# Row maxima of both heads in one VectorE operation, and both sink columns in one write, in a block of four attentions

## The chip, the cores and the metric

The kernel runs on one core of a Trainium2 chip. A core has a matrix engine (TensorE, PE in the profile; its weight loads are PEld), a vector engine (VectorE, DVE), a scalar engine (ScalarE, ACT), a general engine (GpSimd, POOL) and a queue that starts transfers (SyncE, SP). The engines run their own lists of instructions and meet through semaphores: a wait names a semaphore and a count, and other engines' instructions add to it as they end. PSUM is the memory that TensorE writes, eight banks of 512 float32 for each of 128 partitions. The metric is the device time of one execution in microseconds (us), the median of several.

## The reference

Two transformer blocks on 512 tokens of width 1024, in float32. Cut to the attentions, which are what the change touches, and to how the blocks are chained:

```python
# first block
p = jax.nn.softmax(jnp.where(causal, s, -jnp.inf), axis=-1)      # differential attention
a = p[:, :, 0] - lam * p[:, :, 1]
...
p = masked_softmax(s, m)                                          # NSA: selected blocks, window
o = gb[..., 0:1] * o_cmp + gb[..., 1:2] * o_slc + gb[..., 2:3] * o_win
...
x = x + mixed @ w_out[l]
x = x + jnp.square(jax.nn.relu(h @ w_mlp_up[l])) @ w_mlp_down[l]

# second block
logits = logits + ci[..., :, None] - c_k[..., None, :]            # forgetting attention
p = jax.nn.softmax(jnp.where(causal, logits, -jnp.inf), axis=-1)
h = h + (o * jax.nn.silu(gate)) @ w_out_a[i]
...
sink = broadcast_to(sinks, logits.shape[:-1] + (1,))              # windowed attention with sinks
probs = jax.nn.softmax(jnp.concatenate([logits, sink], axis=-1), axis=-1)[..., :-1]
```

Every softmax subtracts the maximum of its row (one query, one head) before the exponential. In the windowed attention each head has one more logit, its sink, which counts in the maximum and in the sum and is dropped then.

## The kernel before

The kernel is written by hand for each engine, with semaphores between them; the order of instructions on an engine is the order in the code. Between long stretches of weight products (line 1421, three products per tile of a high and a low part) come four attentions: DIFF (8 units), NSA (16 units: 8 pairs of heads, each for selected blocks and for the window), FOX (8 units, forgetting) and SWA (8 units, window of 128 with sinks). A unit is two heads, on 512 queries in four tiles of 128. The tiles are taken from the last (`t` = 3, `idx` = 0) to the first, since the last has the widest rows: 512, 384, 256 and 128 keys in DIFF, NSA and FOX, and 256, 256, 256 and 128 in SWA, plus one sink column.

Each engine has a function `attend(a)`, which runs `step(m, ...)` for a unit `m` through `over_units`: the first three units written out, the middle in a loop of two units a turn, and the rest written out. In one step the engines work on the scores of unit `m` and on the values of the unit before it, `b`. For one tile and both heads:

- TensorE, `scores_of`: the products of queries and keys of both heads into two banks, `PS[:, 2 * (idx % 2) + h]`; then for head 0 and for head 1 the mask product (line 1659), with the decay (line 1655) in FOX and the band (1658) in SWA ahead of it. Each head's last product adds one to `s`. Before a tile it waits for the exponentials of the tile that had the same banks.
- VectorE, `maxima`: for head 0, then for head 1, a wait for `s`, in SWA a write of the head's sink into the column behind the scores (line 975) and a wait for that, and the negated row maximum into `NM` (line 978), which adds one to `mx`.
- ScalarE, `exps` (lines 611 to 616): for each head a wait for `mx` and the exponential into `PB` with the row sum into `LS`; the second one adds one to `e`.
- VectorE, `norms` (line 983): the reciprocals of both heads' sums. GpSimd scales the probabilities with them (line 1369).
- TensorE, `turn_p` (line 1678), a unit later: the scaled probabilities transposed into banks 4 and 5. ScalarE (line 625) and, outside DIFF, VectorE (line 1003) copy them to `PT`, and `values_of` (line 1693 in DIFF, 1698 in the others) multiplies them with the values into bank 6.
- For the next unit, `turn` (line 1712) transposes queries and keys into bank 7, ScalarE rounds them (line 633), VectorE takes the rest (line 1008). In FOX and SWA VectorE gates a finished output (line 1026), ScalarE rounds it (line 638), and VectorE takes the rest (line 1032).

The order in a step, which decides who waits for whom: TensorE has scores 3, values 0 of the unit before `b`, transposes 3 of `b`, scores 2, values 3, transposes 2, scores 1, queries of the next unit, values 2, transposes 1, keys of the next unit, scores 0, values 1, transposes 0. ScalarE has exponentials 3, in FOX and SWA the rounding of an output, copies 3 and 2 of `b`, exponentials 2, rounding of queries, exponentials 1, copy 1, rounding of keys, exponentials 0, copy 0. VectorE has maxima 3, the finished output, reciprocals 0 and copy 3 of `b`, maxima 2, reciprocals 3, copy 2, the rest of an output, maxima 1, reciprocals 2, rest of queries, copy 1, maxima 0, rest of keys, reciprocals 1, copy 0.

## Time and profile before

| | us |
|---|---|
| three runs | 1947.2, 1955.84, 1944.85 |
| their median | 1947.2 |
| the profiled execution's own time | 1947.98 |
| its span, from the first to the last instruction | 1946.2 |
| busy in the span: PE / DVE / ACT / POOL | 1759.8 / 892.9 / 705.7 / 366.0 |
| mean granted clock of TensorE | 0.94 |
| DIFF (from 222 to 317 us) | 95 |
| NSA's attention in units (from 595 to 777 us) | 182 |
| FOX (from 1487 to 1609 us) | 122 |
| SWA (from 1790 to 1890 us) | 100 |

The last four rows are stretches of the profiled execution's span that I cut at the first and last score product of each attention. "Busy" is time in which an engine works on an instruction; a row's idle time is what the engine stood before its instructions, with the engine and line whose end released it. A granted clock of 1.00 is TensorE's level of 2.4 GHz, 0.50 that of 1.2 GHz.

### The profile page before, as it was taken

Reading aid. Unit: us, or ns where it says so; the run is one execution under the profiler, and the core shown is the slowest. Engines: PE = TensorE matmul, PEld = TensorE weight load, DVE = VectorE, ACT = ScalarE, POOL = GpSimd, SP = SyncE. Lnnn points to the kernel's source line nnn. Section 1 sums busy time; section 2 is a strip of 40 time slices with the busy share of each in tenths; the row PEclk is TensorE's granted clock in tenths of the full one; section 3 lists DMA queues with packets and bytes.
Section 4 is the critical chain, followed back from the end, with each engine's and each line's share of the span. In section 5 each row is a group of like instructions: output and inputs, shape, how many; then the busy total and the mean of one; then the engine's idle time right before and its main releaser. Section 6 shows DMA issues by size and latency. Waiting matters only on the chain.

```text
span 1946.2 us, 24116 instructions
## 1 busy us (share of the span) xinstructions
PE 1759.8 (90%) x8846; PEld 1348.3 (69%) x8846; DVE 892.9 (46%) x1569; ACT 705.7 (36%) x1525; POOL 366.0 (19%) x490
## 2 busy tenths in 40 slices
PE   2999888999978998997999999989998998798878
PEld 2888656887664554886888888868775546686547
DVE  2485274224544665344342234231662653353661
ACT  3322365122135666323341233132323552433550
POOL 4251042102213655010000000000111440020320
PEclk9999797999987999999999999989998998898899
DMA  5223222323102221432223232322222112132211
GB/s 128 85 87 122 73 76 65 108 87 108 44 12 52 58 67 30 153 108 87 66 89 105 88 107 87 108 65 86 87 82 71 55 34 88 64 108 68 63 41 68
DMA packets 148049, 154.85 MB, mean 80 GB/s; under 512 B 48972, under 2 KB 90172, under 8 KB 147960
## 3 DMA queue, kind: packets, MB, share of 16 engines
q1 hardware_dynamic: 141768, 152.74, 24.8%
q0 software_dynamic: 992, 0.86, 0.3%
q10 hardware_dynamic: 5200, 0.02, 0.3%
q8 instruction: 61, 1.00, 0.2%
q14 instruction: 28, 0.23, 0.0%
HBM read 123.15 MB, written 2.15 MB: 64 GB/s over the span
## 4 chain that ended last, share of the span: by engine, by line
PE 83%; DVE 7%; ACT 6%; issue 3%; ACTq 1%; POOL 0%; DVEq 0%; POOLq 0%
PE ps L1421 61%; PE ps L1649 4%; PE ps L1678 3%; PE ps L1698 3%; PE ps L1712 2%; ACT pb L614 2%; PE ps L1659 2%; DVE qkt L1008 1%; ACTq L476 1%; DVE nm L978 1%; ACT qkt L633 1%; PE ps L1655 1%; PE ps L1549 1%; PE ps L1519 1%; PE ps L1620 1%
## 5 line engine op out<-in xcount | busy, mean ns | idle before, releaser
L1421 PE MATMUL ps<-spl,ht 128*128 128x512 f32 x2496 | 583.0, 396 | 31.5 <-DVE spl L787 16.3
L1421 PEld LDWEIGHTS ps<-spl,ht 128*128 128x128 f32 x2496 | 477.8, 192 | 135.0 <-issue 13.6
L787 DVE TENSOR_TENSOR spl<-raw,spl 128x1024 fp32r<-128x1024 f32 x196 | 253.5, 1336 | 568.5 <-ACT spl L494 568.5
L494 ACT ACTIVATE spl<-raw 128x1024 fp32r<-128x1024 f32 x196 | 196.3, 1052 | 640.0 <-PE ps L1421 639.1
L1421 PE MATMUL ps<-ht,spl 128*128 128x512 f32 x1536 | 351.8, 391 | 2.0 <-DVE spl L787 2.0
L1421 PEld LDWEIGHTS ps<-ht,spl 128*128 128x128 f32 x1536 | 289.9, 189 | 63.2 <-issue 2.9
L614 ACT ACTIVATE pb<-ps,nm 128x512 f32<-128x512 f32 (+5 forms) x320 | 161.4, 513 | 85.9 <-DVE nm L978 85.9
L978 DVE TENSOR_REDUCE nm<-ps 128x1 f32<-128x512 f32 (+5 forms) x320 | 140.0, 467 | 81.9 <-PE ps L1659 78.7
L1421 PE MATMUL ps<-spl,uu 128*128 128x512 f32 x768 | 174.4, 389 | 0.0
L1421 PEld LDWEIGHTS ps<-spl,uu 128*128 128x128 f32 x768 | 144.1, 188 | 29.9
L1649 PE MATMUL ps<-qkt 64*128 64x256 f32 (+2 forms) x960 | 126.4, 372 | 15.8 <-issue 7.0
L1331 POOL TENSOR_TENSOR sq<-qkv 128x2048 f32<-128x2048 f32 (+1 forms) x15 | 51.5, 3435 | 451.2 <-ACT qkv L528 436.6
L1678 PEld LDWEIGHTS ps<-idf,pb 128*128 128x128 f32 x672 | 74.9, 144 | 62.4 <-issue 51.2
L1369 POOL TENSOR_TENSOR pb<-pb,rr 128x256 f32<-128x256 f32 (+3 forms) x128 | 81.5, 660 | 191.3 <-DVE rr L983 191.2
L1649 PEld LDWEIGHTS ps<-qkt 64*128 64x128 f32 x960 | 80.0, 208 | 49.5 <-issue 40.8
L1369 POOL TENSOR_TENSOR pb<-pb,rg 128x512 f32<-128x512 f32 (+3 forms) x160 | 112.8, 721 | 7.5
L1698 PE MATMUL ps<-pt,stv 128*64 128x256 f32 (+3 forms) x512 | 94.1, 446 | 20.3 <-ACT pt L625 11.0
L1678 PE MATMUL ps<-idf,pb 128*128 128x128 f32 x672 | 109.9, 289 | 0.0
L625 ACT ACTIVATE pt<-ps 128x256 f32<-128x256 f32 (+3 forms) x160 | 67.8, 424 | 86.5 <-PE ps L1678 86.1
L1008 DVE TENSOR_TENSOR qkt<-ps,qkt 128x512 fp32r<-128x512 f32 x80 | 54.9, 686 | 94.6 <-ACT qkt L633 94.6
L1421 PE MATMUL ps<-ys,spl 128*128 128x512 f32 x384 | 88.9, 394 | 0.0
L1379 POOL MEMSET nws<- 128x2048 f32 x2 | 3.6, 1807 | 440.0 <-PE ps L1421 440.0
(244 smaller groups left out, 1562.8 us busy)
## 6 DMA issues: line engine op xcount, KB each, us to landing
raw<-w_in SPq DMA_DIRECT2D x30, 1024.0 KB, 5.2
raw<-w_mlp_up SPq DMA_DIRECT2D x16, 1024.0 KB, 5.2
raw<-w_mlp_down SPq DMA_DIRECT2D x16, 1024.0 KB, 5.1
raw<-w_in_a SPq DMA_DIRECT2D x16, 1024.0 KB, 5.3
stq<-qkv SPq DMA_DIRECT2D x56, 256.0 KB, 2.7
raw<-w_in_b SPq DMA_DIRECT2D x8, 1024.0 KB, 5.1
stq<-qkv SPq DMA_DIRECT2D x48, 128.0 KB, 2.5
raw<-w_proj_diff SPq DMA_DIRECT2D x4, 1024.0 KB, 5.1
```

Of the source, the lines that this page charges most:

```text
L494: act.activation(SPL[:, n % 2, HI, 2 * k:2 * k + 2], RAW[:, n % 2, 2 * k:2 * k + 2], ACT.Copy).then_inc(hi_done, 1)
L614: last = act.activation(p, PS[:, 2 * (idx % 2) + h, 0:w], ACT.Exp, bias=NM[:, m.slot, h, t:t + 1], accum_out=LS[:, m.slot, h, t:t + 1])
L625: act.activation(PT[odd][:, 0 if a.is_diff else idx % 2, 0:w], PS[:, 4 + odd, 0:w], ACT.Copy)\
L787: dve.tensor_tensor(SPL[:, n % 2, LO, 2 * k:2 * k + 2], RAW[:, n % 2, 2 * k:2 * k + 2], SPL[:, n % 2, HI, 2 * k:2 * k + 2].bitcast(F32), A ...
L978: dve.tensor_reduce(top, bank[:, 0:w + a.sink], AX.X, ALU.max, negate=True).then_inc(s["mx"], 1)
L1008: dve.tensor_tensor(QKT[:, m.slot, i, LO], PS[:, 7], QKT[:, m.slot, i, HI].bitcast(F32), ALU.subtract)\
L1331: pool.tensor_tensor(SQ[:, :, 0:w], QKV[:, :, col:col + w], QKV[:, :, col:col + w], ALU.mult)\
L1369: last = pool.tensor_tensor(p, p, by[:, m.slot, h, t:t + 1].to_broadcast([P, w]), ALU.mult)
L1421: last = pe.matmul(PS[:, b0 + b], left[:, x], right[:, y], start=(kt == 0 and i == 0), stop=(kt == UK * g["units"] - 1 and i == 2))
L1649: pe.matmul(PS[:, 2 * (idx % 2) + h, 0:w], QKT[r, m.slot, 0, x, P * t:P * t + P], QKT[r, m.slot, 1, y, P * a.first_key(t):P * t + P], star ...
L1678: last = pe.transpose(bank[:, P * i:P * i + P], PB[:, m.slot, h, o:o + P], IDF[:])
L1698: last = pe.matmul(PS[HD * h:HD * h + HD, 6, cols], STV[:, m.slot, j, v], PT[h][:, idx % 2, 0:w], start=(idx == 0 and not (a.is_nsa and m. ...
```

## The change

`maxima` waits once, for the scores of both heads, writes both sinks with one operation (two columns in two banks), and takes both maxima with one reduction over a 128 x 2 x w view of the two banks, into two places of `NM`. `mx` counts one for each step instead of two. `exps` waits once, ahead of both exponentials. TensorE's wait for the last maxima of an attention counts accordingly.

```diff
@@ ScalarE, exps
                     w = a.width(t) + a.sink
+                    act.wait_ge(s["mx"], 4 * m.n + idx + 1)
                     for h in range(2):
-                        act.wait_ge(s["mx"], 8 * m.n + 2 * idx + h + 1)
                         p = PB[:, m.slot, h, a.offset(t):a.offset(t) + w]
@@ VectorE, maxima
                     w = a.width(t)
-                    for h in range(2):
-                        n = 8 * m.n + 2 * idx + h + 1
-                        bank, top = PS[:, 2 * (idx % 2) + h], NM[:, m.slot, h, t:t + 1]
-                        dve.wait_ge(s["s"], n)
-                        if a.is_swa:
-                            dve.tensor_scalar(bank[:, w:w + 1], SINK[:, bass.ds(2 * m.n + h, 1)], 1.0, None, ALU.mult)\
-                               .then_inc(sink_in, 1)
-                            dve.wait_ge(sink_in, n)
-                        dve.tensor_reduce(top, bank[:, 0:w + a.sink], AX.X, ALU.max, negate=True).then_inc(s["mx"], 1)
+                    n = 4 * m.n + idx + 1
+                    banks = PS[:, 2 * (idx % 2):2 * (idx % 2) + 2]
+                    dve.wait_ge(s["s"], 8 * m.n + 2 * idx + 2)
+                    if a.is_swa:
+                        dve.tensor_scalar(banks[:, :, w], SINK[:, bass.ds(2 * m.n, 2)], 1.0, None, ALU.mult)\
+                           .then_inc(sink_in, 1)
+                        dve.wait_ge(sink_in, n)
+                    dve.tensor_reduce(NM[:, m.slot, :, t], banks[:, :, 0:w + a.sink], AX.X, ALU.max, negate=True)\
+                       .then_inc(s["mx"], 1)
@@ TensorE, banks_left
-                pe.wait_ge(s["mx"], 8 * a.units)
+                pe.wait_ge(s["mx"], 4 * a.units)
```

The lists of TensorE, GpSimd and SyncE are the same in both kernels. Each row below is one instruction; REGISTER_ALU and ISA rows are the sequencer's own work for counts and addresses in a loop.

ScalarE at the start of a turn of NSA's loop, from the exponentials of tile 3 (128x512) over the copies of the unit before (L625) to the exponentials of tile 2:

```order
-L612 ISA
-L614 ACTIVATE pb,ls<-ps,nm 128x512
-L612 REGISTER_ALU
-L614 ACTIVATE pb,ls<-ps,nm 128x512
-L622 REGISTER_ALU
-L625 ACTIVATE pt_66<-ps 128x128
...
+L611 ISA
+L614 ACTIVATE pb,ls<-ps,nm 128x512 x2
+L622 REGISTER_ALU
+L625 ACTIVATE pt_66<-ps 128x128
```

The wait between the two exponentials is gone, and the one ahead of the first is for both heads; the copy still follows behind both.

VectorE at the same place, from the maxima of tile 3 to the finished output (L1018):

```order
 L332 UNCONDITIONAL_BRANCH
 L332 ISA
-L978 TENSOR_REDUCE nm<-ps 128x1
-L973 REGISTER_ALU
-L978 TENSOR_REDUCE nm<-ps 128x1
+L977 TENSOR_REDUCE nm<-ps 128x2
 L1015 ISA
 L1018 ISA
```

Two reductions of one row each have become one of two rows.

VectorE in SWA's loop, from the rest of an output (L1032) over the maxima of tile 1 to the reciprocals (L983) and the rest of the queries (L1007, L1008):

```order
 L1032 TENSOR_TENSOR ht<-yt,ht 128x512
-L973 REGISTER_ALU
-L975 TENSOR_SCALAR ps<-sink 128x1
-L978 TENSOR_REDUCE nm<-ps 128x1
-L973 REGISTER_ALU
-L975 TENSOR_SCALAR ps<-sink 128x1
-L978 TENSOR_REDUCE nm<-ps 128x1
-L982 REGISTER_ALU
+L972 REGISTER_ALU
+L974 TENSOR_SCALAR ps<-sink 128x2
+L976 REGISTER_ALU
+L977 TENSOR_REDUCE nm<-ps 128x2
```

Four instructions of VectorE have become two.

## Rows read from the trace of the kernel before

**Rows 1.** The page's costliest groups: busy us, mean ns | idle before, releaser

```profile
L978 DVE TENSOR_REDUCE nm<-ps 128x1 f32<-128x512 f32 (+5 forms) x320 | 140.0, 467 | 81.9 <-PE ps L1659 78.7
```

**Rows 2.** Stretches: PE, PEld, DVE, ACT, POOL busy; clock; DMA; GB/s

```profile
249.84:298.96 49.12, 41.66 (x290) 26.80 (x291) 37.95 (x96) 34.55 (x110) 20.56 (x40) 1.00 0.26 78
660.63:734.71 74.08, 71.62 (x533) 41.66 (x534) 51.24 (x130) 48.40 (x155) 44.33 (x84) 1.00 0.25 62
1531.55:1581.69 50.14, 50.03 (x338) 27.79 (x338) 34.36 (x81) 30.60 (x93) 23.99 (x32) 1.00 0.21 61
1821.82:1875.50 53.68, 43.89 (x379) 27.44 (x380) 39.29 (x141) 33.26 (x115) 21.51 (x40) 1.00 0.21 52
```

**Rows 3.** VectorE's reductions by shape: busy us, mean ns of one

```profile
L978 DVE TENSOR_REDUCE nm<-ps 128x1 f32<-128x512 f32 x64 | 41.4, 687 | 26.4 <-PE ps L1659 26.3
L828 DVE TENSOR_REDUCE ss<-sq 128x16 f32<-128x1024 f32 x3 | 3.6, 1212 | 1.8 <-POOL sq L1331 1.8
L1214 DVE TENSOR_REDUCE lc<-ps 128x16 f32<-128x512 f32 x4 | 2.8, 692 | 8.5 <-PE ps L1589 8.4
```

**Rows 4.** Timeline of one NSA unit: start, us, engine, line [idle before, releaser]

```profile
662.74 1.29 DVE L978 TENSOR_REDUCE nm<-ps 128x1 f32<-128x512 f32 x2 [0.36 <-PE ps L1659]
663.46 0.69 ACT L614 ACTIVATE pb<-ps,nm 128x512 f32<-128x512 f32 x1 [1.18 <-DVE nm L978]
...
664.81 0.27 ACT L625 ACTIVATE pt<-ps 128x128 f32<-128x128 f32 x1
...
665.05 1.02 DVE L978 TENSOR_REDUCE nm<-ps 128x1 f32<-128x384 f32 x2 [0.59 <-PE ps L1659]
665.13 0.20 PEld L1698 LDWEIGHTS ps<-pt,stv 128*64 128x64 f32 x4 [0.24 <-ACT pt L625]
...
666.48 0.58 ACT L614 ACTIVATE pb<-ps,nm 128x384 f32<-128x384 f32 x1
```

**Rows 5.** Timeline of one DIFF unit, the same place

```profile
290.53 1.29 DVE L978 TENSOR_REDUCE nm<-ps 128x1 f32<-128x512 f32 x2 [0.82 <-PE ps L1659]
...
292.92 0.49 PE L1693 MATMUL ps<-pt,stv 128*128 128x128 f32 x2 [0.41 <-ACT pt L625]
```

**Rows 6.** Timeline of one FOX unit, the same place

```profile
1558.79 0.23 PE L1659 MATMUL ps<-causal,idb 128*128 128x128 bf16 x1
...
1559.06 1.29 DVE L978 TENSOR_REDUCE nm<-ps 128x1 f32<-128x512 f32 x2 [0.68 <-PE ps L1659]
...
1559.27 0.23 PE L1659 MATMUL ps<-causal,idb 128*128 128x128 bf16 x1
...
1561.58 0.63 ACT L638 ACTIVATE ht<-yt 128x512 f32 x1 [0.35 <-DVE yt L1026]
...
1562.43 0.20 PEld L1698 LDWEIGHTS ps<-pt,stv 128*64 128x64 f32 x4
```

**Rows 7.** Timeline of one SWA unit, from its third step to the next one's first

```profile
1843.51 0.15 DVE L975 TENSOR_SCALAR ps<-sink 128x1 f32 x1
...
1843.70 0.43 DVE L978 TENSOR_REDUCE nm<-ps 128x1 f32<-128x257 f32 x1
...
1844.57 0.16 DVE L983 RECIPROCAL rr<-ls 128x2 f32<-128x2 f32 x1
...
1846.71 0.16 DVE L975 TENSOR_SCALAR ps<-sink 128x1 f32 x1 [1.06 <-PE ps L1659]
...
1847.51 0.68 DVE L1008 TENSOR_TENSOR qkt<-ps,qkt 128x512 fp32r<-128x512 f32 x1
...
1849.48 0.16 DVE L975 TENSOR_SCALAR ps<-sink 128x1 f32 x1 [0.90 <-PE ps L1659]
...
1850.54 0.68 DVE L1026 TENSOR_TENSOR yt<-ps,mx 128x512 f32<-128x512 f32 x1
...
1850.66 0.48 ACT L614 ACTIVATE pb<-ps,nm 128x257 f32<-128x257 f32 x1
...
1851.37 0.63 ACT L638 ACTIVATE ht<-yt 128x512 f32 x1
```

## The prediction

> **What bounds the kernel now.** I read the page first, then the table of stretches, then the timeline inside each of the four attentions. On the page the reader is to see that the 320 row maxima take 140 us of VectorE and that VectorE sat idle 81.9 us before them, nearly all of it for TensorE's scores [rows 1]: they are taken as soon as their input is there, so what they wait for and who waits for them decides, not their sum. The edit touches only the four attentions: so what must be read is which engine ends the wait last in one unit (two heads) of each. The table of stretches gives steady pieces of them [rows 2]: five units of the first attention (differential) in 49.12 us, 9.8 us each; seven of the second (NSA) in 74.08, 10.6 each; four of the third (forgetting) in 50.14, 12.5 each; five of the fourth (windowed with sinks) in 53.68, 10.7 each. The granted clock is 1.00 in all of them. TensorE is busy 85%, 97%, 99.8% and 82% of these stretches, VectorE 77%, 69%, 69% and 73%. VectorE is full in none; what it does late still counts where others wait for it.
>
> **How a unit runs.** For each of its four query tiles TensorE makes the scores of both heads, VectorE takes the row maximum of head 0 and then of head 1, and ScalarE raises head 0 as soon as its own maximum is there. In the NSA unit shown, the pair of 512-wide reductions starts at 662.74 and takes 1.29 us together; the first exponential starts at 663.46, 0.72 us after the pair began; 1.35 us later, at 664.81, ScalarE copies the transposed probabilities of the unit before; TensorE stood waiting for that copy until 665.13 [rows 4]. So this step of the widest tile is on the path: head 1's maximum is hidden behind head 0's exponential, head 0's isn't hidden by anything. In the differential attention the same rows read alike: the pair starts at 290.53, and TensorE waits 0.41 us for the same copy, until 292.92 [rows 5].
>
> **What the change does, part by part.** Each of the four steps of a unit loses one reduction (320 become 160 [rows 1]), and the last attention also loses 32 of its 64 sink writes. Both exponentials of a step now wait for one count, that of the joint reduction, and this in turn waits for the scores of head 1.
>
> *The price of the joint reduction.* No row of before shows 2 x 512 elements of PSUM reduced in one operation. A reduction of 1024 elements in 16 rows from SBUF takes 1.212 us; 512 elements in 16 rows from PSUM take 0.692, and 512 in one row from PSUM 0.687 [rows 3], so neither rows nor source matter much. I take 1.21 us. That is 0.08 less than the 1.29 of the pair, since the pair already overlaps. The bounds are 0.69 (both banks read at once, which no row suggests) and 1.37 (two full reductions in a row).
>
> *Differential and NSA, widest tile.* Before, 0.72 us from the start of the pair to the first exponential. Now 1.21, plus the 0.03 between the end and the exponential, plus 0.05 for the second head's scores, which come right behind the first's (an estimate, between 0 and 0.1): 1.29. Everything behind it moves by 0.57 us, and the waits in front of TensorE [rows 4, 5] say that no slack takes it up. With 16 and 8 units: 24 x 0.57 = 13.7 us. The next tile costs nothing: its pair, begun at 665.05, is wholly done at 666.07, and ScalarE comes to its exponentials only at 666.48 [rows 4]; the 256-wide tile is alike. Of the 128-wide one the pair is so short that its exponentials start about 0.15 later (two maxima of 128 cost less than one of 384), and what they release isn't waited for.
>
> *Forgetting attention.* It looks safe, since TensorE is never idle. But its two heads' scores aren't done together: the causal product of head 0 starts at 1558.79, that of head 1 at 1559.27, 0.48 us apart, as the decay is added to each head between them [rows 6]. The joint reduction so starts 0.48 later and the exponentials 0.48 + 1.21 + 0.03 - 0.72 = 1.00 us later. Against it stands ScalarE's slack: exponentials that began 0.72 after 1559.06 are over 1.35 later, at 1561.13, and the next item, the rounding of the gated output, began only at 1561.58 because it waited for VectorE: 0.45 us. Behind it TensorE takes the copy at 1562.43 with no idle time, but the copy had not been done much earlier (the rounding starts at 1561.58 and takes 0.63, and the copy follows it), so I give it no slack. 1.00 - 0.45 = 0.55; I take 0.6, as other units may have less slack in ScalarE, for six units: 3.6. For the first two units, in which the pipeline still fills, 0.2 each, an estimate between 0 and 0.6. Sum 4.0 us.
>
> *Sink attention.* Here VectorE sets the pace in stretches, so the change gives something back. Tile 1, third step of a unit: sink write at 1843.51, reduction at 1843.70, the next operation at 1844.57, so 1.06 us [rows 7]; now 0.19 for the sink write and 0.69 - 0.08 for 514 elements, 0.80: 0.26 less, of which I count 0.24, since the rounding it is followed by waits for ScalarE. Tile 0, fourth step: 1846.71 to 1847.51, 0.80; now 0.05 + 0.19 + 0.34 = 0.58: 0.22 less. Tile 3, first step of the next unit: sink write at 1849.48, gated output at 1850.54; VectorE gains 0.2, but the exponentials now start at 1849.48 + 0.05 + 0.19 + 0.69 + 0.03 = 1850.44 and last 2 x 0.48, until 1851.40, where before ScalarE went on at 1851.37 (its second exponential had started at 1850.66): ScalarE takes the gain away, 0. The second step, tile 2, is covered on both sides. 0.46 for six steady units is 2.8 us less; 0.1 goes back in the first unit, where the exponentials are on the path: -2.7.
>
> **The sum.** 13.7 + 4.0 - 2.7 = +15.0 us. The profiled execution took 1947.98 us with a span of 1946.2; the median of the runs is 1947.2. From the first it gives 1963.0, from the second 1962.2. I say 1962.
>
> **The skill.** The Trainium skill, page "Perfetto Trace Analysis", section "Optimizing Scalar/DVE Operations", gives VectorE about 125 ns of access overhead for each instruction on PSUM and says that grouping can improve throughput if the engine is saturated; 192 instructions fewer would be 24 us less by that estimate. [Rows 2] don't have VectorE saturated, and the pair of reductions already hides most of that overhead. The same section of the Trainium skill says that where the engine isn't saturated but makes others wait, breaking up instructions may let work finish sooner. The change is the reverse of that, and the trace agrees with this second rule by the waits in [rows 4, 5].
>
> **The rivals.** *Grouping pays everywhere (faster).* If VectorE were the bound in all four attentions, each pair would save 0.08 us and each sink step 0.26: 32 units x 4 x 0.08 = 10.2 and 32 x 0.24 = 7.7 (an average over its steps), so 1929. It decides where VectorE has no idle time before the reductions; against it, VectorE is idle for 0.36 us before the pair in [rows 4] and 0.82 in [rows 5]. Chance 0.03.
>
> *The delay is hidden (not slower).* If ScalarE's copy had 0.57 us of slack to TensorE at the widest tile, the 13.7 and the 4.0 would be gone and only the sinks' gain left: 1945. It decides from a slack of 0.57; for it, TensorE's own wait is only 0.24 and 0.41 us, so a second thing may be nearly as late, and a later start can find cover that a single unit doesn't show; a reduction at its lower bound of 0.69 gives the same result. Against it, TensorE stands waiting in both places. Half hidden, it gives 1954. Chance for both 0.13.
>
> *The clock falls.* More idle time in TensorE could bring back its lower level (1.2 GHz) in the middle of an attention. One NSA unit at it would cost up to TensorE's busy time in it, 71.62 / 7 = 10.2 us. It decides where the granted clock of [rows 2] falls below 1.00; against it, the differential and the sink attention keep 1.00 with TensorE idle 15% and 18%. Result 1975 or more, chance 0.04.
>
> **How the numbers follow.** Forecast 0.80: 1957 to 1970, with the reduction between 1.2 and 1.37 us (30 x 0.16 = 4.8 more) and the forgetting attention between 0 and 6. The range that leaves out under 2 in 10 is 1955 to 1970. A measurement of this kernel tells about 0.5%, 9.7 us, from no change: faster (under 1937.5) 0.03; within (up to 1956.9) 0.13; slower 0.84.
>
> **What would show it.** In the profile after, one 128x2 reduction of about 1.21 us for 2 x 512; the first exponential 1.29 us behind the moment where the pair began; steady units of 10.4, 11.15, 13.1 and 10.3 us; in the forgetting attention a new wait of TensorE for the copy; clock 1.00. The forecast is wrong if the steady NSA unit stays at 10.6, if the joint reduction takes far from 1.21, or if the sink units don't shorten.

## The result: slower by 27 us, 12 more than forecast

| | median us | runs |
|---|---|---|
| kernel before | 1948.97 | 4 (1944.85 to 1955.84) |
| changed kernel | 1975.66 | 4 (1974.07 to 1980.41) |

The ratio is 1.0137 with a 95% interval from 1.0102 to 1.0172: 26.7 us slower. The forecast said slower, 1962 us, range 1955 to 1970. The side was right, the size was not. The two profiled executions took 1947.98 and 1980.41 us, 32.4 us apart, more than the medians; the mean granted clock of TensorE was 0.940 and 0.930. I read places and unit lengths from them, and total times from the medians.

The page of the kernel before and then that of the changed kernel, costliest groups (columns as in [rows 1]):

```profile
L614 ACT ACTIVATE pb<-ps,nm 128x512 f32<-128x512 f32 (+5 forms) x320 | 161.4, 513 | 85.9 <-DVE nm L978 85.9
```

```profile
L614 ACT ACTIVATE pb<-ps,nm 128x512 f32<-128x512 f32 (+5 forms) x320 | 160.6, 511 | 119.9 <-DVE nm L977 116.8
...
L977 DVE TENSOR_REDUCE nm<-ps 128x2 f32<-128x1024 f32 (+5 forms) x160 | 125.8, 786 | 105.5 <-PE ps L1659 104.0
...
L1698 PE MATMUL ps<-pt,stv 128*64 128x256 f32 (+3 forms) x512 | 96.9, 457 | 33.4 <-ACT pt L625 24.6
```

VectorE's maxima cost 125.8 us where [rows 1] had 140.0, and it now stands idle 105.5 before them for 81.9. The exponentials wait 116.8 us for it, where they waited 85.9 before. Before TensorE's products with the values stand 24.6 us of idle time that a copy of ScalarE ended (11.0 on the page of the kernel before). VectorE works less and is waited for more.

By shape, the new operations:

```profile
L977 DVE TENSOR_REDUCE nm<-ps 128x2 f32<-128x1024 f32 x32 | 39.2, 1226 | 32.3 <-PE ps L1659 32.3
...
L977 DVE TENSOR_REDUCE nm<-ps 128x2 f32<-128x514 f32 x24 | 16.7, 695 | 0.8
...
L974 DVE TENSOR_SCALAR ps<-sink 128x2 f32<-128x2 f32 x16 | 2.6, 163 | 12.9 <-PE ps L1659 12.8
```

The joint reduction of 1024 elements takes 1.226 us (forecast 1.21), that of 2 x 257 takes 0.695.

Steady stretches of the changed kernel (columns as in [rows 2]): four units of DIFF, twelve of NSA, three of FOX, four of SWA:

```profile
262.82:304.40 41.58, 33.29 (x232) 21.44 (x233) 29.23 (x61) 27.02 (x88) 16.37 (x32) 1.00 0.25 72
643.65:777.88 134.23, 122.79 (x913) 71.55 (x912) 85.28 (x174) 82.82 (x264) 76.50 (x145) 1.00 0.23 57
1573.71:1613.31 39.60, 37.67 (x254) 20.86 (x254) 24.20 (x48) 22.58 (x69) 18.11 (x25) 1.00 0.17 50
1855.78:1898.15 42.37, 35.34 (x305) 22.15 (x305) 28.34 (x80) 25.85 (x92) 17.20 (x32) 1.00 0.25 63
```

Divided by their units: 10.40, 11.19, 13.20 and 10.59 us. Units of before, from first scores product to first scores product, are 9.83, 10.59, 12.54 and, as a mean of the same four, 10.86. So a steady unit grew by 0.57, 0.60 and 0.66 us and shrank by 0.27 in SWA. Over the units for which the forecast counted them (8, 16, 6, 6) this is 4.6 + 9.6 + 4.0 - 1.6 = 16.5 us, for which the prediction had 15.0. The longer and shorter units therefore explain 16.5 of the 26.7 us; about 10 are something else.

Where they are is seen when each attention is cut as a whole, from its first transpose of queries to the first weight product behind it. (The stretches of 95, 182, 122 and 100 us in the table ahead of the prediction were said to be cut at the first and last score product. They aren't: from first to last score product it is 77.8, 168.3, 101.1 and 83.6 us.) First before, then after, in the order DIFF, NSA, FOX, SWA:

```profile
222.26:317.12 94.86, 75.33 (x465) 47.65 (x465) 61.02 (x152) 58.15 (x179) 33.25 (x64) 0.87 0.21 62
590.94:778.74 187.80, 170.96 (x1217) 99.55 (x1217) 119.25 (x298) 114.66 (x356) 101.33 (x192) 0.95 0.22 54
1485.78:1612.87 127.09, 109.78 (x673) 60.16 (x673) 72.86 (x175) 67.35 (x191) 47.11 (x64) 0.88 0.16 47
1788.21:1892.67 104.46, 78.55 (x608) 49.65 (x609) 66.16 (x226) 58.24 (x188) 34.41 (x64) 0.88 0.19 46
```

```profile
222.99:325.34 102.35, 78.24 (x465) 49.21 (x465) 59.22 (x120) 57.54 (x179) 33.28 (x64) 0.84 0.20 57
601.96:800.44 198.48, 172.00 (x1216) 100.53 (x1217) 115.34 (x234) 114.52 (x356) 101.91 (x192) 0.94 0.21 51
1507.20:1644.21 137.01, 115.70 (x673) 63.85 (x673) 68.24 (x143) 66.43 (x191) 47.39 (x64) 0.84 0.15 43
1819.76:1925.68 105.92, 80.85 (x608) 50.35 (x609) 59.31 (x162) 56.49 (x188) 34.40 (x64) 0.83 0.19 45
```

The four together are 29.5 us longer, of 32.4 in these two executions, so nearly all of it lies inside the attentions. Each is longer than its steady units account for: DIFF by 7.5 (4.6 expected from the units), NSA by 10.7 (9.6), FOX by 9.9 (4.0), SWA by 1.5 (-1.6); together 13 us. And in each the granted clock is lower. A clock of 0.84 over 137 us, with only 1.00 and 0.50 as levels, is 2 x 0.16 x 137 = 44 us at the lower one. Summed in this way, the four have 99 us at the lower level before and 136 after, both to some 5 us, since the clocks are given to 0.01. The same work with the same number of instructions keeps PE busy for 5.9 us longer in FOX (115.70 for 109.78), which is that lower clock seen in the busy time. If TensorE were the bound all the while, 37 us more at half speed would cost 18.5 us; at the start and the end of an attention it isn't, so as an estimate 18.5 is an upper bound for the 13.

FOX shows one such place. Its units start, in the changed kernel, 14.3, 19.0, 15.9 and then 13.2 us apart; before 13.8, 16.2 and then 12.5. Slices of 4 us from the end of the second unit over the third (1544.67 to 1560.53), changed kernel:

```profile
1542.00:1546.00 4.00, 4.00 (x20) 2.24 (x16) 1.32 (x3) 1.40 (x5) 1.18 (x2) 0.69 0.25 69
1546.00:1550.00 4.00, 3.55 (x19) 1.44 (x18) 2.49 (x5) 2.04 (x6) 0.76 (x2) 1.00 0.22 66
1550.00:1554.00 4.00, 3.86 (x24) 2.40 (x26) 2.47 (x6) 1.65 (x7) 2.55 (x3) 0.66 0.01 4
1554.00:1558.00 4.00, 4.00 (x20) 2.85 (x20) 1.25 (x2) 2.54 (x7) 1.55 (x2) 0.50 0.00 0
1558.00:1562.00 4.00, 4.00 (x27) 2.21 (x25) 1.79 (x4) 1.41 (x5) 1.19 (x2) 0.98 0.45 133
```

TensorE had come up to its higher level by 1546. Then it waited once, 0.59 us for ScalarE's copy until 1550.14 (0.45 of it in one slice, 0.14 in the next). The clock fell to 0.50 some 1.2 us behind the end of that wait, while TensorE was busy again without a break. It then did 20 products in 4 us where it does 27 in the last slice. So it was up for good only at 1558, 51 us behind the attention's start (1507). Before the change it came up once, some 30 us behind the start (1486), and stayed up:

```profile
1510.00:1514.00 4.00, 4.00 (x21) 2.56 (x22) 1.79 (x5) 1.51 (x5) 2.04 (x2) 0.50 0.00 0
1514.00:1518.00 4.00, 4.00 (x26) 2.50 (x24) 1.44 (x5) 2.54 (x7) 1.61 (x2) 0.72 0.00 0
1518.00:1522.00 4.00, 4.00 (x26) 2.15 (x27) 2.44 (x6) 1.41 (x5) 1.18 (x2) 1.00 0.48 133
```

The other 7 us lie elsewhere. In DIFF and NSA 0.9 and 1.1 us are in the first two units, mostly the second (12.93 for 11.59 and 14.41 for 12.72). DIFF and SWA lose most in their last part, behind the last score product: DIFF's takes 14.43 us at a clock of 0.78 for 12.23 at 1.00. SWA's, in the kernel before, in the changed one, and in the kernel that is changed in NSA alone:

```profile
1876.47:1892.67 16.20, 7.19 (x51) 3.74 (x51) 7.75 (x20) 7.63 (x19) 3.12 (x6) 0.97 0.00 1
```

```profile
1907.02:1925.68 18.66, 9.70 (x51) 4.66 (x51) 7.20 (x16) 7.54 (x19) 3.12 (x6) 0.66 0.01 1
```

```profile
1891.08:1910.32 19.24, 10.23 (x51) 5.02 (x51) 7.75 (x20) 7.63 (x19) 3.11 (x6) 0.63 0.01 1
```

The third has SWA's code as before, and the same loss. This place has two lengths: 16.2 to 16.4 us in seven of the fourteen profiles of this document and 18.0 to 19.2 in the other seven, and either kind has kernels with the change in SWA and without. FOX's second unit is alike, as said below. So of the 13 us, 5.3 (2.8 in FOX's second unit, 2.5 in SWA's last part) can't be put down to the edit at that place. They may be an effect of shifted work, or of the execution that was profiled.

The waits themselves, timelines of one unit of the changed kernel (start, us, engine, line, [idle before, releaser]). NSA, the place of [rows 4]:

```profile
667.25 1.23 DVE L977 TENSOR_REDUCE nm<-ps 128x2 f32<-128x1024 f32 x1 [0.42 <-PE ps L1659]
...
668.51 0.69 ACT L614 ACTIVATE pb<-ps,nm 128x512 f32<-128x512 f32 x1 [1.77 <-DVE nm L977]
...
669.85 0.27 ACT L625 ACTIVATE pt<-ps 128x128 f32<-128x128 f32 x1
...
670.37 0.44 PE L1698 MATMUL ps<-pt,stv 128*64 128x128 f32 x4 [0.84 <-ACT pt L625]
```

The exponential starts 1.26 us after the reduction began (0.72 before), and TensorE's wait for the copy is 0.84 us where [rows 4] had 0.24. In DIFF it is 1.00 where [rows 5] had 0.41. FOX, the place of [rows 6]:

```profile
1588.12 0.23 PE L1659 MATMUL ps<-causal,idb 128*128 128x128 bf16 x1
...
1588.60 0.23 PE L1659 MATMUL ps<-causal,idb 128*128 128x128 bf16 x1
...
1588.87 1.23 DVE L977 TENSOR_REDUCE nm<-ps 128x2 f32<-128x1024 f32 x1 [1.16 <-PE ps L1659]
...
1590.13 0.69 ACT L614 ACTIVATE pb<-ps,nm 128x512 f32<-128x512 f32 x1 [2.51 <-DVE nm L977]
...
1591.47 0.62 ACT L638 ACTIVATE ht<-yt 128x512 f32 x1
...
1592.31 0.44 PE L1698 MATMUL ps<-pt,stv 128*64 128x128 f32 x4 [0.54 <-ACT pt L625]
```

The reduction starts 0.27 us after head 1's causal product began, 0.75 after head 0's. ScalarE no longer stands idle before the rounding (0.35 us in [rows 6]), and TensorE, which waited for nothing here before, waits 0.54 us. It is this wait that comes with the falls of the clock in the middle of FOX.

### The profile page after: what moved, and what is told of

The parts are those of the page before. It is cut to its first block, busy times and chain, and to the rows that moved or that the text cites. A ratio compares the mean times of both kernels' runs of the same rounds, so it can differ in the third digit from the quotient of the medians.

```text
span 1978.6 us, 23670 instructions
## 1 busy us (share of the span) xinstructions
PE 1774.5 (90%) x8846; PEld 1358.7 (69%) x8846; DVE 875.7 (44%) x1377; ACT 702.3 (35%) x1525; POOL 366.9 (19%) x490
## 4 chain that ended last, share of the span: by engine, by line
PE 80%; ACT 8%; DVE 7%; issue 3%; ACTq 1%; POOL 0%; DVEq 0%; POOLq 0%
PE ps L1421 60%; PE ps L1649 4%; ACT pb L614 3%; PE ps L1678 3%; PE ps L1698 3%; DVE nm L977 2%; PE ps L1712 2%; DVE qkt L1008 1%; ACTq L476 1%; PE ps L1659 1%; ACT qkt L633 1%; PE ps L1693 1%; PE ps L1549 1%; PE ps L1519 1%; PE ps L1620 1%
## 5 line engine op out<-in xcount | busy, mean ns | idle before, releaser
L614 ACT ACTIVATE pb<-ps,nm 128x512 f32<-128x512 f32 (+5 forms) x320 | 160.6, 511 | 119.9 <-DVE nm L977 116.8
L977 DVE TENSOR_REDUCE nm<-ps 128x2 f32<-128x1024 f32 (+5 forms) x160 | 125.8, 786 | 105.5 <-PE ps L1659 104.0
L1649 PE MATMUL ps<-qkt 64*128 64x256 f32 (+2 forms) x960 | 127.7, 376 | 16.5 <-issue 6.7
L1698 PE MATMUL ps<-pt,stv 128*64 128x256 f32 (+3 forms) x512 | 96.9, 457 | 33.4 <-ACT pt L625 24.6
L1678 PE MATMUL ps<-idf,pb 128*128 128x128 f32 x672 | 114.0, 298 | 0.0
L625 ACT ACTIVATE pt<-ps 128x256 f32<-128x256 f32 (+3 forms) x160 | 67.8, 424 | 84.7 <-PE ps L1678 84.7
L1008 DVE TENSOR_TENSOR qkt<-ps,qkt 128x512 fp32r<-128x512 f32 x80 | 54.9, 687 | 95.3 <-ACT qkt L633 94.8
L1003 DVE COPY pt<-ps 128x256 f32<-128x256 f32 (+3 forms) x128 | 58.9, 460 | 66.7 <-PE ps L1678 66.1
```

What stands on the lines that cost most here:

```text
L614: last = act.activation(p, PS[:, 2 * (idx % 2) + h, 0:w], ACT.Exp, bias=NM[:, m.slot, h, t:t + 1], accum_out=LS[:, m.slot, h, t:t + 1])
L625: act.activation(PT[odd][:, 0 if a.is_diff else idx % 2, 0:w], PS[:, 4 + odd, 0:w], ACT.Copy)\
L977: dve.tensor_reduce(NM[:, m.slot, :, t], banks[:, :, 0:w + a.sink], AX.X, ALU.max, negate=True)\
L1003: dve.tensor_copy(PT[1][:, idx % 2, 0:w], PS[:, 5, 0:w]).then_inc(s["pt_b"], 1)
L1008: dve.tensor_tensor(QKT[:, m.slot, i, LO], PS[:, 7], QKT[:, m.slot, i, HI].bitcast(F32), ALU.subtract)\
L1649: pe.matmul(PS[:, 2 * (idx % 2) + h, 0:w], QKT[r, m.slot, 0, x, P * t:P * t + P], QKT[r, m.slot, 1, y, P * a.first_key(t):P * t + P], star ...
```

## The experiments

Theory A: the waits cost what was forecast, and the rest is TensorE at its lower level for longer, after the starts of the attentions and, in FOX, in the middle of it. Theory B: only the waits (or the operations themselves) cost, and the clock is an accident of the profiled execution. The last parts of DIFF and SWA are in neither. All runs below are timed against runs of the kernel before on the same chip. In the edits, `joint(a, idx)` says whether a step of attention `a` takes the changed form; where it doesn't, the code is that of before.

### One attention at a time

The changed form in DIFF alone, in NSA alone, in FOX alone, in SWA alone:

```diff
-                    for h in range(2):
-                        ...
+                    if joint(a, idx):      # e1: a.is_diff; e2: a.is_nsa; e3: a.is_fox; e4: a.is_swa
+                        dve.wait_ge(s["s"], 8 * m.n + 2 * idx + 2)
+                        ...
+                        dve.tensor_reduce(NM[:, m.slot, :, t], banks[:, :, 0:w + a.sink], AX.X, ALU.max, negate=True)\
+                           .then_inc(s["mx"], 1)
+                        return
+                    for h in range(2):
+                        ...
```

> The joint reduction in the differential attention only. Two theories: A, the extra wait per unit is what was forecast, and on top of it TensorE, idle longer in an attention's first units, comes back to its upper clock later; B, only the extra wait per unit costs, at the sizes forecast, and the rest of the 27 us lies elsewhere in the program. A: the stretch from the last product before the attention to the first after it grows from 125.9 us by 8 (5 for eight steady units, 3 in the first three), and the run takes +8 us over the kernel before. B: +4.6 us.

> The joint reduction in NSA only. A: +12 us over the kernel before (16 units at 0.59 and 2 to 3 us in the first two). B: +9.1 us.

> The joint reduction in the forgetting attention only. A: +10 us over the kernel before (steady units 13.2 instead of 12.54 us, so 4 for six, and 6 in the first three, where the granted clock stays at 0.50 for 10 us more). B: +4.0 us, with the clock as before.

> The joint reduction and sink write in the sink attention only. A: +1.5 us over the kernel before: steady units 0.27 us shorter, and 3 to 4 us lost at a lower clock in the first units. B: -2.7 us.

| changed form in | us | before | ratio, 95% interval | difference | by steady units |
|---|---|---|---|---|---|
| DIFF | 1956.14 | 1949.53 | 1.0028 [1.0011, 1.0044] | +6.6 | +4.6 |
| NSA | 1962.72 | 1949.53 | 1.0057 [1.0039, 1.0075] | +13.2 | +9.6 |
| FOX | 1961.23 | 1949.53 | 1.0063 [1.0042, 1.0085] | +11.7 | +4.0 |
| SWA | 1951.69 | 1949.53 | 1.0009 [0.9994, 1.0023] | +2.2 | -1.6 |

The differences are those of the medians; by the ratios they are 5.5, 11.1, 12.3 and 1.8 us. Each comes out above its units, but in DIFF and NSA the interval includes what the units give, so these two don't decide between A and B. Their profiles do show the same places as the changed kernel: DIFF's second unit takes 12.8 us and its last part 14.4 (12.0 to 12.3 with DIFF as before), NSA's second unit 14.4. FOX is the clear case, 11.7 us for 4.0, and in its profile the clock falls in units that were steady before. The whole attention, and then its fourth, fifth and sixth unit:

```profile
1483.96:1626.32 142.36, 121.24 (x673) 66.84 (x673) 68.29 (x143) 66.50 (x191) 47.39 (x64) 0.79 0.14 41
```

```profile
1534.64:1551.85 17.21, 16.67 (x86) 9.46 (x85) 8.13 (x16) 7.64 (x23) 6.69 (x10) 0.71 0.19 54
1551.85:1565.12 13.27, 12.64 (x85) 7.01 (x85) 8.05 (x16) 7.53 (x23) 5.39 (x7) 0.99 0.18 52
1565.12:1579.50 14.38, 13.84 (x85) 7.88 (x85) 8.14 (x16) 7.59 (x23) 6.04 (x9) 0.88 0.19 55
```

Three units of the same work take 17.21, 13.27 and 14.38 us with clocks of 0.71, 0.99 and 0.88. The idle time of PE in them is 0.54, 0.63 and 0.54 us: it is the same wait each time, and only sometimes does the clock fall.

The four differences sum to 33.7 us, 7 more than the whole change costs. Part of the excess moves with the kernel rather than with the edit: the step from FOX's second to its third unit took 16.2 us in the kernel before, with DIFF alone changed and with SWA alone changed, but 19.1 with NSA alone changed, where FOX's code is untouched. SWA's last part, 16.2 or 19.2 us, is the other such place, and it is the long one with SWA alone changed, which more than makes up for the shorter units. So a difference of 3 us between two of these kernels can't be put down to the edit. Nor can all of the 7.7 us of FOX: in its profile 5.2 us are falls in the fourth and sixth unit, 2.8 the second unit, and 2.7 the part behind the last scores, which is also 24.8 instead of 21.8 us in a profile with FOX's code as before (the kernel before with fillers, below). The falls can: the ten profiles in which FOX's widest tile is not joint have no such unit from the third on (12.5 to 12.8 us throughout), and the three in which it is, with nothing put into the wait, have units of 15.9, of 17.2 and 14.4, and of 14.4 and 14.4.

### The wait without the operation

The reductions and sink writes stay as before, one for each head. Only ScalarE waits for both maxima ahead of the first exponential:

```diff
                     for h in range(2):
-                        act.wait_ge(s["mx"], 8 * m.n + 2 * idx + h + 1)
+                        if h == 0:
+                            act.wait_ge(s["mx"], 8 * m.n + 2 * idx + 2)
```

> Two reductions and two sink writes as before; only the exponentials of both heads wait for both. If the loss is the first exponential's later start: the differential and NSA units are 0.57 us longer as in the changed kernel (24 units, 14 us), the forgetting ones 0.15, the sink ones 0.4, and with the clock at the starts it comes to +20 us. If the joint operation itself is slow: 0.

Measured 1968.05 us, ratio 1.0105 [1.0083, 1.0127]: 19.0 us of the 26.7, with no operation changed. Steady pieces of it, twelve NSA units and one FOX unit:

```profile
636.22:770.51 134.29, 122.72 (x913) 71.45 (x913) 88.25 (x222) 82.84 (x264) 76.50 (x145) 1.00 0.23 57
```

```profile
1589.61:1602.33 12.72, 12.57 (x85) 6.94 (x85) 8.46 (x20) 7.53 (x23) 6.00 (x9) 1.00 0.10 30
```

NSA's unit is 11.19, exactly that of the changed kernel: there the whole loss is ScalarE's wait for head 1's maximum, and what one operation saves over two is nothing. FOX's unit is 12.7 for the 13.2: of its 0.66 us, 0.2 come from waiting for both maxima. The other 0.5 fit the reduction itself starting only with head 1's scores, which no run separates. The Trainium skill, page "Perfetto Trace Analysis", section "Optimizing Scalar/DVE Operations", says that where an engine isn't saturated but makes others wait, breaking up instructions may let work finish sooner; this run agrees: two maxima that are waited for one by one are worth the 19 us.

### Only the steps that looked free

The other way round: tile 3, the widest, stays apart in all four attentions, and the three narrower steps take the changed form.

```diff
+JOINT = {'diff': (1, 2, 3), 'nsa': (1, 2, 3), 'fox': (1, 2, 3), 'swa': (1, 2, 3)}    # idx = 3 - tile
```

> The joint reduction for tiles 2, 1 and 0 of every unit, the first tile (512 wide, 257 with sinks) with two reductions and two waits as before. If the first tile alone carries the loss: -3 us, the gain in the sink attention, with steady units of 9.8, 10.6, 12.5 and 10.4 us. If every joint reduction costs: half of the 27 us or more remain.

Measured 1952.94 us, ratio 1.0020 [1.0008, 1.0032], +3.9 where -3 was expected. Its steady units are as expected:

```profile
628.33:755.51 127.18, 122.82 (x913) 71.44 (x913) 85.93 (x186) 82.96 (x264) 76.16 (x145) 1.00 0.24 60
```

Twelve NSA units at 10.60 us, as before: the narrow steps cost nothing, as the prediction said. DIFF is at 9.83, and SWA's units are 10.52 for 10.86. FOX as a whole took 130.64 us at a clock of 0.85 against 127.09 at 0.88, though most of its units are no longer. The loss lies in the two places with two lengths: FOX's second unit took 19.1 us for 16.2, and SWA's last part 18.4 for 16.2, which is 5.1 us against some 2 gained in SWA's units. Both are low clock, and this run doesn't show that the edit causes them.

### Keeping TensorE's clock up

If theory A is right, products that compute nothing but fill TensorE's idle time at the start of an attention must make the kernel faster, although they are more work. 36 products of the identity with itself, 128 x 128, go into a bank that is written anew before it is read: 8 behind each of the first two transposes, and 6, 8 and 6 within the first unit (two of these three places are shown).

```diff
+                def fill(place):
+                    for _ in range(WARM.get(place, 0)):
+                        pe.matmul(PS[:, 5, 0:P], IDF[:], IDF[:], start=True, stop=True, skip_group_check=True)
...
+                    if first:
+                        fill("unit0_2")
                     if scores:
                         scores_of(m, 1)
                     if turning:
                         turn(m.after(), 0)
+                    if first:
+                        fill("unit0_q")
...
                 turn(Unit(0, 0, 0), 0)
+                fill("start0")
                 turn(Unit(0, 0, 0), 1)
+                fill("start1")
```

They are added to the kernel before, and to the changed kernel:

> The kernel before, with 36 small products of TensorE in the waits of each attention's first unit (into a bank that nobody reads then), so that it stays busy while queries and keys are made ready. A (the clock makes up the rest of the loss): the low stretches at the start of the four attentions shrink, and the run takes 10 us less than the kernel before. B (the clock's low stretches have nothing to do with it): 0 to +3 us.

> The changed kernel with the same small products. A: over the same kernel without the change (the run beside it) only the steady waits are left, 8 x 0.63 + 16 x 0.59 + 8 x 0.65 - 8 x 0.27 = +17.5 us; so +8 over the kernel before. B: the two differ by 27 us as without the products.

The kernel before with them: 1935.67 us, ratio 0.9921 [0.9898, 0.9943], 13.3 us faster. The changed kernel with them: 1957.84 us, ratio 1.0046 [1.0029, 1.0063]; 17.8 us below the changed kernel's median above, and 22.2 above the other. DIFF and NSA of the first:

```profile
222.33:314.12 91.79, 77.02 (x536) 52.71 (x537) 61.13 (x152) 57.86 (x179) 33.27 (x64) 0.98 0.22 64
590.37:773.96 183.59, 171.75 (x1289) 103.57 (x1289) 119.07 (x298) 114.20 (x356) 101.31 (x192) 1.00 0.23 55
```

NSA's clock goes from 0.95 to 1.00 and its stretch from 187.80 to 183.59 us with 36 more products in it (each is two records, so 72). DIFF's clock goes from 0.87 to 0.98 and its stretch from 94.86 to 91.79. FOX went from 127.09 to 124.89 and SWA from 104.46 to 103.13. That speaks against theory B, which has no room for a gain from added work.

In the changed kernel the fillers at the starts do not reach the falls in the middle of FOX. The attention as a whole, and its fourth unit:

```profile
1489.83:1625.55 135.72, 119.13 (x745) 70.37 (x745) 68.45 (x143) 66.33 (x191) 47.38 (x64) 0.88 0.15 44
```

```profile
1536.83:1551.23 14.40, 13.87 (x86) 7.83 (x86) 8.14 (x16) 7.58 (x23) 6.04 (x9) 0.88 0.20 58
```

It is 10.8 us longer than FOX in the kernel before with fillers (124.89), where the units account for 4.0. Its largest loss is the second unit, 17.9 us for 11.6: TensorE, at 1.00 until then, waits 1.16 us for ScalarE's copy (0.16 in the other), and the clock falls within that wait and stays at 0.50 for 13 us. So the remaining 22.2 us are 17 of waits and some 6 of falls in FOX, if the wait there is what makes them.

### Filling FOX's wait

That is tested by three more such products in each FOX unit, into the bank that the values will write, behind the wait for its last reader and just ahead of the values that wait for ScalarE's copy. They leave the wait of the pipeline as it is and only keep TensorE at work in it.

```diff
                     if values:
+                        if a.is_fox:
+                            reach(pe, s["o"], b.n)
+                            for _ in range(3):
+                                pe.matmul(PS[:, 6, 0:P], IDF[:], IDF[:], start=True, stop=True,
+                                          skip_group_check=True)
                         values_of(b, 3)
```

> The changed kernel with the small products in the first units, and three more (0.5 us) in TensorE's new wait in each unit of the forgetting attention. A (the clock falls in the middle of this attention because of that new wait): no low stretch between its third unit and its last, all steady units at 13.2 us, its stretch 5 to 6 us shorter than in the same kernel without the three, 1952 instead of 1958. B (the falls come from elsewhere): they stay, and the run stays at 1958.

Measured 1946.04 us, ratio 0.9983 [0.9974, 0.9992], 11.8 us below the same kernel without them (1957.84, where the kernel before took 1949.01; here it took 1948.76), twice what I expected. FOX as a whole, and five units in a row:

```profile
1491.48:1617.53 126.05, 114.07 (x793) 69.23 (x793) 67.84 (x143) 66.18 (x191) 47.50 (x64) 0.99 0.16 47
```

```profile
1519.97:1586.52 66.55, 66.09 (x453) 38.06 (x452) 39.80 (x80) 37.68 (x115) 30.26 (x41) 1.00 0.19 54
```

All five take 13.3 us, the clock is 1.00 throughout, and there is no fall left. Unit for unit they are even 0.1 longer than a steady unit of the changed kernel, so the gain is the clock and nothing else. FOX is 9.7 us shorter than without them: 5.3 in the second unit (12.6 us for 17.9), 1.9 net in the steady ones, where two falls are gone, and 2.6 behind the last scores. The last also changes with FOX's code untouched, and so does the second unit with the start fillers (11.6 or 14.3 us), but it was never 17.9 without the wait. So between 4 and 7 us are the filled wait's.

This also gives the cost of the waits nearly by themselves. The same kernel before with the start fillers, run again beside this one:

> The kernel before with the small products again, to compare the other three with on one chip: 14 us less than the kernel before, as in its first run (1935.7).

Measured 1929.04 us, ratio 0.9914 [0.9892, 0.9935], most runs at a mean clock of 0.964 to 0.966, where the run above has 0.964. With the mean clock equal, the change costs 1946.04 - 1929.04 = 17.0 us. The steady units give 16.5, the prediction 15.0. That these agree so well is in part luck: the kernel before had two kinds of executions here (the lower kind 1927.71 to 1929.30, the higher 1935.51 and 1939.19), and its profile of the lower kind has a fall in FOX's second unit (14.3 us, for 11.6 in the profile of its first run), though TensorE waited only 0.15 us there.

### Is there a version that uses the joint operation?

The narrow steps joint in all four attentions, with the start fillers; and then only in SWA, where VectorE does set the pace, with one sink write for both heads in every step there:

```diff
-JOINT = {}
-SINKS_JOINT = False
+JOINT = {'swa': (1, 2, 3)}
+SINKS_JOINT = True
```

> Joint reductions for tiles 2, 1 and 0 in all four attentions, the first tile apart, with the small products in the first units. Against the kernel before with the same products (the last run of this set): A (the first tile carries the loss, and the +3.9 us seen without the products came from the clock): -3 us, the sink attention's gain. B (the narrower tiles cost time too): +4 us or more.

> The kernel before with the small products in the first units, and in the sink attention one sink write for both heads in every step and the joint reduction for tiles 2, 1 and 0 only. Both theories: steady sink units of 10.3 instead of 10.8 us, so 3 us less than the kernel before with the products alone (the last run of this set): 1933.

The first: 1930.98 us, ratio 0.9916 [0.9899, 0.9932], 1.9 above the kernel before with fillers of the same set. Theory B's loss isn't there, and theory A's gain of 3 isn't seen in the median either. Beside the profile of the kernel before with fillers from the same set, SWA takes 2.1 us less from its first score product to its last, and its last part 2.3 us more (18.5 for 16.2): the gain is there and is hidden by the place with two lengths. The second: 1936.78 us, ratio 0.9917 [0.9893, 0.9942]. Its SWA, five steady units:

```profile
1813.27:1865.00 51.73, 43.91 (x383) 27.45 (x384) 35.52 (x107) 32.26 (x114) 21.50 (x40) 1.00 0.22 54
```

10.35 us here, 10.43 as the mean of four against 10.81 in the other: the gain in SWA is real, 0.38 us a unit, some 2 us in all. The medians don't show it, because executions of one and the same kernel lie at 1928 or at 1937 us with mean clocks of 0.964 or 0.957. Of the ones at the higher clock, its two took 1924.99 and 1927.71, those of the kernel without it 1927.71 to 1929.30. This is some 2 us and isn't settled.

None of these is clearly better than the kernel before with the start fillers alone, which is 0.8 to 0.9% faster than before and, by its two medians (1935.67 and 1929.04), 2.0 and 2.4% faster than the changed kernel.

## Why the prediction was right about the side and wrong about the size

- **The price of the operation** was right: 1.21 us forecast, 1.226 measured; the pair had cost 1.29. So was the choice between the bounds.
- **DIFF and NSA, 0.57 us a unit** was right: 0.57 and 0.60. TensorE's wait grew from 0.24 to 0.84 us and from 0.41 to 1.00, so there was no slack, as those waits said (the 0.24 is read from the weight load, the others from the product behind it; in the changed kernel the two started within 0.03 us of each other). That the narrower tiles cost nothing holds too (NSA 10.60 with only these joint).
- **FOX, 0.6 us a unit** was right with 0.66, and so were its two causes, the later start and the use of ScalarE's slack; the run with the wait alone has 0.2 of it. The term for its first two units, 0.2 us each, was mis-sized: they took 3.3 us more together (14.3 + 19.0 for 13.8 + 16.2), though the same 2.9 us in the second of them also came with NSA alone changed. The third (15.9 for 12.5, of which a steady unit explains 0.7) has the other 2.7 of the 5.9 us that FOX grew beyond its units: there the clock fell again.
- **SWA, 0.46 us a unit less** was too much: 0.27. The operations are as short as forecast (in the changed kernel 0.80 us from sink write to the next operation in tile 1, 0.54 in tile 0), but what they free is partly given back as idle time before the next scores. The three places in the changed kernel:

```profile
1877.74 0.17 DVE L974 TENSOR_SCALAR ps<-sink 128x2 f32 x1 [1.12 <-PE ps L1659]
...
1878.28 0.68 DVE L1008 TENSOR_TENSOR qkt<-ps,qkt 128x512 fp32r<-128x512 f32 x1
...
1880.36 0.16 DVE L974 TENSOR_SCALAR ps<-sink 128x2 f32 x1 [1.00 <-PE ps L1659]
...
1885.24 0.16 DVE L974 TENSOR_SCALAR ps<-sink 128x2 f32 x1
...
1886.04 0.16 DVE L983 RECIPROCAL rr<-ls 128x2 f32<-128x2 f32 x1
```

  VectorE is idle 1.12 and 1.00 us for TensorE where [rows 7] have 1.06 and 0.90. That and the rest made -1.6 us of the forecast -2.7; the error is small. SWA as a whole is even 1.5 us longer, by its last part.
- **The step that failed is the clock, which the sum put at nothing**: it has no term for time at the lower level, the rival "the clock falls" had a chance of 4%, and "clock 1.00" stood among what the profile after would show. The runs showed some 10 of the 26.7 us beyond the longer units, and time at the lower level grown from 99 to 136 us in the profiles; filling the wait in FOX tied the falls there to the change, DIFF's and NSA's places came back with that attention alone changed, and for 5.3 us of the 13 in the profiles the cause stays open. The rival's time of 1975 or more is what came, but not by its working, so that the number fits is in part luck. Two things in it were wrong. I looked for it in NSA, one unit of 10.2 us at a time, and it came in FOX, in the second units of DIFF and NSA, and in the last parts of DIFF and SWA. And I took as evidence against it that the differential and the sink attention keep 1.00 with TensorE idle 15% and 18%. That is true and still so in [rows 2] and after, but it doesn't carry over to a unit that had no idle time and gets one short wait: FOX fell to 0.50 with 5% idle time. I also read only the steady stretches. The whole attentions of before had clocks of 0.87, 0.95, 0.88 and 0.88, so some 99 us at the lower level were there to be seen, and with DIFF or NSA alone changed the second unit grew by 1.2 and 1.7 us where a steady one grew by 0.6. A term for that belonged in the sum, or at least in the upper end of the range.
- **The range** ended at 1970 because the clock had been left out. The waits alone, 17.0 us with the mean clock kept equal, would have given 1966 from 1948.97, within it.

What stays open: why the same 0.54 us of idle time is followed by a fall in one FOX unit and not in the next, and how much of the low clock outside FOX's steady units comes from the change and how much varies with anything that shifts the work (3 us in FOX's second unit and 3 in SWA's last part with their code untouched). In FOX, filling the wait showed that the falls there are the wait's. For the starts of the other attentions the fillers show that clock is time there, not that the change alone lengthened it. No run was made on the last parts.

## What to carry to other kernels

Joining two operations into one saves the fixed part of one, but what waited for the first of the two now waits for both (0.6 us later for two rows of 512): before joining, look whether the consumer starts between the two, and whether TensorE waits for that consumer. Where VectorE isn't full, a joint reduction was worth nothing, and the delay was worth 0.6 us a unit. When a change adds a wait to an engine that had none, look at the granted clock of the whole phase, not of its steady middle, and if it is low, try a few products that compute nothing in the idle places: here 36 of them for each attention took 0.8% off the kernel, and 3 in each unit of FOX took a further 12 us off the changed one. And before a difference of a few us is put down to an edit, compare the places that it doesn't touch: two of them here had two lengths, 3 us apart.

## What the runs showed of the hardware that was not expected

- TensorE's granted clock fell from 1.00 to 0.50 (2.4 to 1.2 GHz) in FOX after waits of some 0.5 us in a stream otherwise full, and once, in the kernel before with fillers, after one of 0.15, while it stayed at 1.00 in DIFF with 20% idle time after the change (33.29 us busy in 41.58).
- Added work made the kernel faster: 36 products that compute nothing at the start of each attention, 1949.01 to 1935.67 us and, run again, 1948.76 to 1929.04, the mean clock from 0.94 to 0.957 or 0.965.
- The length of a unit with the same work follows the clock: in FOX 13.27, 14.38 and 17.21 us at 0.99, 0.88 and 0.71.
- The reductions from PSUM took the same time for the same number of elements in one row or two: 0.695 us for 2 x 257 beside 0.687 for one row of 512 [rows 3]; 2 x 512 took 1.226. A sink write of two columns in two banks takes 0.163 us, of one 0.155.
- The same place of unchanged code took one of two times: SWA's part behind the last scores 16.2 us at a clock of 0.97 or 19.2 at 0.63, FOX's second unit 16.2 or 19.1 us. Two profiled executions of one kernel (that of before with fillers) had 18.0 and 16.2 in the first and 11.6 and 14.3 in the second.
